# Modulation tiles ahead of a unit's sums, the next weight tile's split behind its second, and RMS statistics that go along with their sums

## Chip, cores and metric

One NeuronCore of a Trainium2 chip runs the whole program. The metric is the device time of one execution in microseconds (us). The kernel before took 2876.29 us, the median of three runs (2874.13 to 2876.8).

## What is computed

Two transformer layers over 512 latent tokens and 256 context tokens of width 1024, then a third layer of another kind (gated linear attention, mLSTM, S5 and a gated feed-forward). Only the first two layers matter here. Everything is float32 at the interface.

```python
for i in range(2):
    mod_lat = silu(c) @ w_ada[i] + b_ada[i]        # 6 x 1024, for x
    mod_ctx = silu(c_ctx) @ w_ada[i] + b_ada[i]    # 6 x 1024, for xc
    h_lat = x * (1 + sc_a) + sh_a;  h_ctx = xc * (1 + csc_a) + csh_a
    # i == 0: q, k, v = split(h @ w_qkv); q, k rms-normed by head, rotated
    # i == 1: cq, ckv, k_pe = split(h @ w_in)
    #         q = rms_norm(cq) @ w_uq;  k, v = rms_norm(ckv) @ w_ukv
    x = layer_norm(alpha * x + g_a * (attention(...) @ w_o))
    x = layer_norm(alpha * x + g_m * (relu(modulated(x) @ w1) ** 2 @ w2))
    # the same two lines for xc where i == 0
```

The third layer's modulation, `silu(c_2) @ ada_w_2`, is computed beside the MLPs of the first two.

## The kernel before

Activations lie with features on the partitions and tokens in the columns, in segments: segment 0 is the 512 latent tokens, segment 1 the 256 context tokens, 2 and 3 are the halves of segment 0. The layer norms go by thirds of 256 tokens, p = 2, 3, 1 in this order.

**Products.** A float32 product is made of three bf16 products (`mm3`, lines 288 to 290): both operands are split into a high and a low bf16 half. Weights come in tiles of 1 MB, [128, 8 x 256]. `load_tiles` (SyncE, line 250) issues their DMAs in the order in which TensorE uses the tiles, into two staging slots of `WS`. `high_halves` (ScalarE, line 274) copies a tile to bf16, `low_halves` (VectorE, line 284) makes the difference, into two pairs of buffers `WB`. A DMA into a slot waits until the tile two places before it has been used up: for a weight tile that is its low half (`dve_done`), for a modulation tile the matmuls on it (`pe_done`).

**Units.** `sums` (line 299) walks through the units of a product. A unit is one weight tile, two blocks of 128 output features; each block has a sum per segment, 8 x 3 matmuls of 512 or 256 columns. With both segments a unit is four sums, with segment 0 alone two. After each sum `then` is called, where other work of TensorE stands.

**Modulation tiles.** `w_ada` is 3 x 8 tiles of 1 MB per layer, [128, 2048], used in float32 straight from the staging slot (`ada_pe`, line 487): four matmuls each. They are laid beside other products by `BESIDE` (line 529): two tiles per unit in the q, k, v product, in `wo0` and in the first MLP's first product `("w1", 0)`, one per unit in `("w1", 1)`. `beside_pe` uses one behind the unit's first sum and one behind its second. When eight tiles are summed, ScalarE copies the rows (`ada_act`, line 496), TensorE transposes them (`ada_turn_pe`, line 502, behind the sum after the last tile) and VectorE adds the bias (line 512).

**Places of the splits.** `next_tiles(tag, i)` names the first weight tile behind unit i. ScalarE and VectorE ask for it before they touch the unit's first sum: in the q, k, v product (`first` in `qkv_act` and `qkv_dve`, ScalarE's square at line 685), and in the MLP (`mlp_act`, relu at 1365 and square at 1367; `mlp_dve`, lines 1377 and 1380). VectorE also computes small tables for the third layer there, one piece behind each sum (`beside(e)` of `mlp_dve`, `tables_dve`). GpSimd fills larger ones from them and stores each with a DMA (`e_scratch`).

**Output products with layer norm.** `wo0`, `w20`, `wo1`, `w21` (attention output and second MLP product of layers 0 and 1) go through `out_sums_pe`, `out_sums_act`, `out_sums_dve`. Their last unit (features 6 and 7) goes by thirds. For each third, `late(p)` and `final(p)` add up mean and mean square in TensorE (lines 1052 to 1064), which need VectorE's `gate(6, p)` and `gate(7, p)` (line 1204). `first_sums_pe` is the first unit of the product that follows; it goes by thirds too, k by k as VectorE delivers the modulated inputs.

**Compressed q, k, v.** `mla_in_pe` makes the sums of cq (three), ckv (four) and k_pe (two). Then it rotates k_pe (`rope_pe`, line 1656) and sums the squares of the seven blocks with a matrix of ones (line 1566). ScalarE turns each of the three sums into a root (lines 1590 and 1592), VectorE scales (line 1611) and splits (line 1615). The next product's first part `qpe` needs the three blocks of cq; ScalarE's `rope_act` (line 1664) starts each of its rotations.

```python
BESIDE = {"qkv": ([("ada0", t) for t in range(8, 16)], 2, 4, "side5"),
          "wo0": ([("ada0", t) for t in range(16, 24)], 2, 4, "side5"),
          ("w1", 0): ([("ada1", t) for t in range(24)] + [("ada2", t) for t in range(8)], 2, 4, "side"),
          ("w1", 1): ([("ada2", t) for t in range(8, 24)], 1, 2, "side")}
```

Of the kernel before, what the change touches and what calls it, by code (L numbers as in the profile page):

```python
# [129 lines left out]
def build(nc, a, out):  # L130
    ctx = ExitStack()
    with ctx:
# [166 lines left out]
        def sums(e, tag, src, units, nks, rhs, segs, then=None, whole=False, ring="dense", first=0):  # L299

            for i, (c0, nc_, ms) in enumerate(units):
# [221 lines left out]
        def first_mods_dve(e):  # L523
# [5 lines left out]
        BESIDE = {"qkv": ([("ada0", t) for t in range(8, 16)], 2, 4, "side5"),  # L529
                  "wo0": ([("ada0", t) for t in range(16, 24)], 2, 4, "side5"),  # L530
                  ("w1", 0): ([("ada1", t) for t in range(24)] + [("ada2", t) for t in range(8)], 2, 4, "side"),
                  ("w1", 1): ([("ada2", t) for t in range(8, 24)], 1, 2, "side")}

        def beside_sum(stage, n):

            if stage not in BESIDE:
                return None, None
            ts, per, sums, _ = BESIDE[stage]
            unit, r = divmod(n, sums)
            name, t = ts[unit * per + per - 1] if unit * per < len(ts) else (None, 0)  # L540
            return ts[unit * per + r] if name and r < per else None, (name, t // 8) if r == per and t % 8 == 7 else None
# [8 lines left out]
        def beside_act(e, stage, n):  # L550
            tile_, _ = beside_sum(stage, n)
            if tile_ and tile_[1] % 8 == 7:
                ada_act(e, tile_[0], tile_[1] // 8)

        def beside_dve(e, stage, n):
            _, whole = beside_sum(stage, n)
            if whole:
                ada_dve(e, *whole)
# [68 lines left out]
        def qkv_pe(e):  # L627
# [13 lines left out]
            def then(e, key, s):  # L641
                u = QU.index((key, s))
                if u > 1:
                    swap(u - 2)
                if u > 0:
                    head(u - 1)
                beside_pe(e, "qkv", u)
# [2443 lines left out]
```

## Time and profile before

| | |
|---|---|
| median of three runs | 2876.29 us |
| profiled execution, its own time | 2874.26 us |
| span of its trace | 2872.5 us |
| mean granted TensorE clock | 0.962 |
| TensorE busy | 2607.8 us, 91% |
| VectorE, ScalarE, GpSimd busy | 50%, 36%, 26% |
| HBM | 92 GB/s over the span |

The profile is one execution. "Busy" for TensorE counts overlapping matmuls once, with modelled ends. The clock is a share of 2.4 GHz. A row of the timeline is "start, duration, engine, line, operation", and in brackets how long the engine had been idle before it and which instruction released it. Such stretches lie, in us of the span: q, k, v product 58 to 232; attention 0 to 449; `wo0` to 533; first MLP's first product to 848 (its first unit is that by thirds), its second to 1118; compressed q, k, v to 1175; attention 1 with its heads to 1436; `wo1`, second MLP to 1827; the third layer to the end.

### The profile page before, as it was taken

The numbers are of one execution on the slowest core, as the hardware profiler recorded it, in microseconds if no ns is written. First come the engines' busy times: TensorE is split into PE (matmuls) and PEld (weight loads), VectorE is DVE, ScalarE is ACT, GpSimd is POOL, SyncE is SP. The second block draws the span as 40 slices with busy tenths as digits, with TensorE's granted clock in tenths as the row PEclk, the third lists the DMA queues.
The fourth block names the chain that finished last, engine by engine and source line by source line (L and its number), as shares of the span: only waits on it lengthen the run. The fifth ranks groups of instructions, "written<-read, shape, count | busy, mean of one in ns | idle before, by whom it ended". The sixth has DMA issues, their size and how long they took to land.

```text
span 2872.5 us, 39059 instructions
## 1 busy us (share of the span) xinstructions
PE 2607.8 (91%) x16373; PEld 1442.9 (50%) x16584; DVE 1445.7 (50%) x2179; ACT 1041.1 (36%) x1713; POOL 743.6 (26%) x985
## 2 busy tenths in 40 slices
PE   4789999889999998889999999887898998899997
PEld 1346665645556576357654445544543333344443
DVE  2336884773342125688664422665765653433322
ACT  2335773333231113567543322322342213422221
POOL 1220000248787722400040000033253543011100
PEclk7899999999999999999999999999989999999998
DMA  6220003345552221210035532221112323233321
GB/s 222 103 88 16 2 2 118 115 160 189 197 176 84 93 75 49 67 59 2 30 118 186 189 109 90 78 96 52 52 52 73 99 70 110 59 103 103 99 96 55
DMA packets 206078, 268.26 MB, mean 93 GB/s; under 512 B 8975, under 2 KB 188558, under 8 KB 196686
## 3 DMA queue, kind: packets, MB, share of 16 engines
q1 hardware_dynamic: 199758, 243.97, 26.5%
q0 software_dynamic: 5280, 18.64, 1.8%
q8 instruction: 130, 2.13, 0.3%
q10 hardware_dynamic: 864, 3.15, 0.3%
q14 instruction: 46, 0.38, 0.0%
HBM read 252.62 MB, written 10.49 MB: 92 GB/s over the span
## 4 chain that ended last, share of the span: by engine, by line
PE 69%; DVE 16%; ACT 5%; issue 3%; POOL 3%; DMA 3%; SPq 0%; POOLq 0%; DVEq 0%; ACTq 0%
PE PS L289 19%; PE PS L288 19%; PE PS L290 19%; DVE WB L284 2%; PE PS L487 2%; PE PS L851 2%; DVE SM L933 2%; DVE AR L939 2%; ACT WB L274 1%; DMA WS<-in_mlp_w 1%; DMA WS<-in_gqa_w_qkv 1%; DVE X L1216 1%; DVE GT L1225 1%; PE PS L632 1%; PE PS L1999 1%
## 5 line engine op out<-in xcount | busy, mean ns | idle before, releaser
L289 PE MATMUL PS<-H,WB 128*128 128x512 bf16 (+1 forms) x1953 | 686.2, 351 | 30.5 <-DVE WB L284 10.5
L288 PE MATMUL PS<-H,WB 128*128 128x512 bf16 (+2 forms) x1907 | 668.2, 350 | 25.5 <-DVE WB L284 13.7
L290 PE MATMUL PS<-H,WB 128*128 128x512 bf16 (+2 forms) x1949 | 683.5, 351 | 1.2
L284 DVE TENSOR_TENSOR WB<-WS,WB 128x2048 bf16<-128x2048 f32 (+3 forms) x165 | 375.5, 2276 | 583.4 <-ACT WB L274 583.3
L274 ACT ACTIVATE WB<-WS 128x2048 bf16<-128x2048 f32 (+3 forms) x165 | 295.5, 1792 | 663.5 <-PE PS L290 424.9
L288 PE MATMUL PS<-AR,WB 128*128 128x512 bf16 (+1 forms) x1279 | 431.6, 337 | 15.8 <-DVE WB L284 7.6
L289 PE MATMUL PS<-AR,WB 128*128 128x512 bf16 (+1 forms) x1280 | 431.7, 337 | 8.1 <-DVE AR L1615 4.8
L290 PE MATMUL PS<-AR,WB 128*128 128x512 bf16 (+1 forms) x1281 | 431.7, 337 | 1.1
L288 PEld LDWEIGHTS PS<-H,WB 128*128 128x128 bf16 x1976 | 194.4, 98 | 298.5 <-issue 65.2
L290 PEld LDWEIGHTS PS<-H,WB 128*128 128x128 bf16 x1976 | 195.2, 99 | 176.4 <-issue 9.2
L289 PEld LDWEIGHTS PS<-H,WB 128*128 128x128 bf16 x1976 | 194.9, 99 | 165.5 <-issue 7.7
L1304 POOL TENSOR_TENSOR X<-X,STAT 128x256 f32<-128x256 f32 x56 | 47.1, 877 | 710.8 <-DVE H L1233 710.8
L288 PEld LDWEIGHTS PS<-AR,WB 128*128 128x128 bf16 x1300 | 127.9, 98 | 135.8 <-issue 13.8
L290 PEld LDWEIGHTS PS<-AR,WB 128*128 128x128 bf16 x1300 | 127.9, 98 | 98.8 <-issue 2.5
L289 PEld LDWEIGHTS PS<-AR,WB 128*128 128x128 bf16 x1300 | 127.9, 98 | 97.3 <-issue 3.3
L939 DVE TENSOR_TENSOR AR<-PS,AR 128x384 bf16<-128x384 f32 x288 | 143.9, 535 | 18.0 <-ACT AR L899 16.8
L933 DVE TENSOR_REDUCE SM<-PS 128x1 f32<-128x768 f32 x160 | 135.5, 848 | 24.4 <-PE PS L290 21.8
L899 ACT ACTIVATE AR<-PS 128x384 bf16<-128x384 f32 x288 | 124.4, 477 | 57.1 <-PE PS L851 55.7
L289 PE MATMUL PS<-AR 128*128 128x64 bf16 (+3 forms) x736 | 142.9, 245 | 2.4 <-ACT STAT L892 0.9
L290 PE MATMUL PS<-AR 128*128 128x64 bf16 (+3 forms) x736 | 142.9, 245 | 0.0
L288 PE MATMUL PS<-AR 128*128 128x64 bf16 (+3 forms) x705 | 131.7, 240 | 4.8 <-ACT AR L892 2.1
L1204 DVE SCALAR_TENSOR_TENSOR X<-PS,MOD,X 128x256 f32<-128x256 f32 (+1 forms) x56 | 33.5, 597 | 189.9 <-PE PS L290 189.9
(399 smaller groups left out, 3781.3 us busy)
## 6 DMA issues: line engine op xcount, KB each, us to landing
WS<-in_mlp_w SPq DMA_DIRECT2D x64, 1024.0 KB, 5.6
WS<-in_w_ada SPq DMA_DIRECT2D x48, 1024.0 KB, 5.0
WS<-in_w_in SPq DMA_DIRECT2D x26, 1024.0 KB, 5.1
WS<-in_ada_w SPq DMA_DIRECT2D x24, 1024.0 KB, 4.9
WS<-in_ffn_w_in SPq DMA_DIRECT2D x44, 512.0 KB, 4.8
e_scratch<-EB POOLq DMA_DIRECT2D x16, 512.0 KB, 3.7
EB<-e_scratch POOLq DMA_DIRECT2D x16, 512.0 KB, 3.6
WS<-in_ffn_w_out SPq DMA_DIRECT2D x8, 1024.0 KB, 5.4
```

Of the source, the lines that this page charges most:

```text
L274: e.activation(halves_of(i)[0], staged(i), COPY).then_inc(ac.sem, ac.mark(("hi", i)))
L284: e.tensor_tensor(lo, staged(i), hi, SUB).then_inc(dv.sem, dv.mark(("lo", i)))
L288: e.matmul(out_, l[0], r[0], start=start, stop=False)
L289: e.matmul(out_, l[0], r[1], start=False, stop=False)
L290: return e.matmul(out_, l[1], r[0], start=False, stop=stop)
L487: m = e.matmul(ps(bank_of[name, "sums", g], 512, slice(32 * j, 32 * j + 32)), SIL[:, pair, k, :], v[:, 0, j * 512:(j + 1) * 512], start=k ...
L851: m = e.transpose(at(("T", t, u, i), 128, (k - a_) * 128), Q.p(u)[:, k * 128:(k + 1) * 128], ident)
L899: e.activation(Q.pt(u, i)[0], Q.turned_at(u, i), COPY).then_inc(ac.sem, ac.mark(("high", t, u, i)))
L933: e.tensor_reduce(Q.largest(u), Q.scores_at(u), AX.X, MAX, negate=True).then_inc(dv.sem, dv.mark(("max", t, u)))
L939: e.tensor_tensor(lo, Q.turned_at(u, i), hi, SUB).then_inc(dv.sem, dv.mark(("low", t, u), ("free", ("T", t, u, i))))
L1204: e.scalar_tensor_tensor(out=seg(X, f, s), in0=ps(bank_of[tag, f, s], SEG[s][1]), scalar=MOD[:, i, (3 * j + 2) * 8 + f, SEG_OF[s]:SEG_OF[s ...
L1304: e.tensor_tensor(seg(X, f, p), seg(X, f, p), factor_at(p), MUL).then_inc(po.sem, po.mark(("over", tag, f, p), ("factor read", tag)))
```

## The change

Six edits:

1. In `sums`, both modulation tiles of a unit are taken and used ahead of its first sum; the transposes of a finished set stand behind the first sum of the same unit. The order of the tiles in the staging slots stays as it was.
2. ScalarE and VectorE split the next weight tile behind the unit's second sum (its first, where a unit has two).
3. In the last unit of `w20`, `wo1` and `w21`, the next tile's split stands ahead of `gate(7)` and of ScalarE's `part_sums`.
4. `late(1)` and `final(1)` of the last third leave `out_sums_pe`; `first_sums_pe` of the next product runs them (`rest`) behind the fourth k of its first third.
5. `gate(6)` of the next third stands behind three of eight `less_mean`, `gate(7)` two features sooner.
6. The seven sums of squares go between the sums of ckv and k_pe; the root of cq, its scaling and its split come behind the fourth block, those of ckv behind the rotation's start.

```diff
@@ sums
                     w, hi, lo = tile(e, (tag, i, c), src[k0 * 128:(k0 + nk) * 128, c0:c0 + nc_], nk, nc_, whole)
+                    if beside and c == 0:
+                        beside_pe(e, beside, i)
@@ BESIDE, helpers
-        def beside_pe(e, stage, n):
-            tile_, whole = beside_sum(stage, n)
-            if tile_:
-                ada_pe(e, *tile_, BESIDE[stage][3])
-            if whole:
-                ada_turn_pe(e, *whole, BESIDE[stage][3])
+        def beside_pe(e, stage, unit):
+            for tile_ in beside_tiles(stage, unit):
+                ada_pe(e, *tile_, BESIDE[stage][2])
+
+        def beside_turn_pe(e, stage, unit):
+            for whole in whole_set(stage, unit):
+                ada_turn_pe(e, *whole, BESIDE[stage][2])
@@ qkv_act, first (qkv_dve likewise)
-                high_halves(e, next_tiles("qkv", key // 2))
+                if u % 4 == 0:
+                    beside_act(e, "qkv", u // 4)
                 pe.wait_ge(e, ("qkv", key, s))
...
                 e.activation(sq, ps(bank_of["qkv", key, s], n), SQUARE).then_inc(ac.sem, ac.mark(("sq", u)))
-                beside_act(e, "qkv", u)
+                if u % 4 == 1:
+                    high_halves(e, next_tiles("qkv", key // 2))
@@ out_sums_pe
-                        if key == 7:
+                        if key == 7 and p != 1:
                             late(p)
                             final(p)
                 k0 += nk
+            def rest(e):
+                if ns > 1:
+                    late(1)
+                    final(1)
+            return rest
@@ first_sums_pe
+                    if p == 2 and k == 3:
+                        rest(e)
@@ out_sums_act
-                high_halves(e, next_tiles(tag, i, last))
-                beside_act(e, tag, n)
+                high_halves(e, through(tag, i, last))
...
+                if n % (2 * len(segs)) == len(segs) - 1:
+                    high_halves(e, next_tiles(tag, i, last))
             high_halves(e, through(tag, 3, last))
+            beside_act(e, tag, 3)
             square(6, P[0])
+            if tag != "wo0":
+                high_halves(e, next_tiles(tag, 3, last))
             part_sums(0)
             square(7, P[0])
@@ out_sums_dve
             gate(6, P[0])
-            gate(7, P[0])
+            beside_dve(e, tag, 3)
             if tag != "wo0":
                 low_halves(e, next_tiles(tag, 3, last))
+            gate(7, P[0])
...
                 for f in range(8):
                     less_mean(f, p)
-                if after:
-                    gate(6, after)
+                    if f == 2 and after:
+                        gate(6, after)
...
-                    if f == 2 and after:
+                    if f == 0 and after:
                         gate(7, after)
@@ mlp_act (mlp_dve likewise)
-                high_halves(e, next_tiles(("w1", i), t))
+                if n % (2 * len(segs)) == 0:
+                    beside_act(e, ("w1", i), t)
...
-                beside_act(e, ("w1", i), n)
+                if n % (2 * len(segs)) == len(segs) - 1:
+                    high_halves(e, next_tiles(("w1", i), t))
@@ mla_in_pe
+            first_sums_pe(e, "cq", WI, CQ[0], (0,), "w20", rest, lambda: None)
             linear(e, "cq", WI, CQ, [8], h_of("w20"), (0,), first=1)
-            linear(e, "ckv", WI, CKV, [8], h_of("w20"), (0, 1))
-            linear(e, "kpe", WI, KPE, [8], h_of("w20"), (0, 1))
+            square(0)
+            square(1)
+            behind = iter(range(2, 6))
+            linear(e, "ckv", WI, CKV, [8], h_of("w20"), (0, 1), lambda e, m, s: square(next(behind)))
+            linear(e, "kpe", WI, KPE, [8], h_of("w20"), (0, 1), lambda e, m, s: square(6) if s == 0 else None)
```

**TensorE, one unit of the first MLP's first product.** L288 to L290 are the sums (512 columns, then 256), L487 before and L489 after the change are the matmuls on modulation tiles. Before:

```order
L290 MATMUL PS<-H,WB 128x512
L487 MATMUL PS<-WS,SIL 32x512 [waits weights1_landed]
L487 MATMUL PS<-WS,SIL 32x512 x3
L288 MATMUL PS<-H,WB 128x256
...
L290 MATMUL PS<-H,WB 128x256
L487 MATMUL PS<-WS,SIL 32x512 [waits weights0_landed]
L487 MATMUL PS<-WS,SIL 32x512 x3
L288 MATMUL PS<-H,WB 128x512 [waits act_done]
```

After:

```order
L290 MATMUL PS<-H,WB 128x256
L489 MATMUL PS<-WS,SIL 32x512 [waits weights0_landed]
L489 MATMUL PS<-WS,SIL 32x512 x3
L489 MATMUL PS<-WS,SIL 32x512 [waits weights1_landed]
L489 MATMUL PS<-WS,SIL 32x512 x3
L288 MATMUL PS<-H,WB 128x512
```

The second modulation tile's wait for its landing moved from behind two sums to ahead of both.

**SyncE, the same stage.** One unit's three loads; these rows read the same before and after.

```order
L263 DMA WS<-in_mlp_w 128x8x256 [waits pe_done]
L263 DMA WS<-in_w_ada 128x2048 [waits pe_done]
L263 DMA WS<-in_w_ada 128x2048 [waits dve_done]
```

The second modulation tile's load waits for VectorE (`dve_done`), whose place in its own program moved.

**ScalarE, the same stage.** L274 is the split, L1365 and L1367 are relu and square before, L1391 and L1393 after. Before:

```order
L274 ACTIVATE WB<-WS 128x2048 [waits weights1_landed]
L1365 ACTIVATE GT<-PS 128x512 [waits pe_done,dve_done]
L1367 ACTIVATE AR<-GT 128x512 [waits act_done]
L1365 ACTIVATE GT<-PS 128x256 [waits pe_done,dve_done]
L1367 ACTIVATE AR<-GT 128x256 [waits act_done]
```

After:

```order
L1391 ACTIVATE GT<-PS 128x512 [waits pe_done,dve_done]
L1393 ACTIVATE AR<-GT 128x512 [waits act_done]
L1391 ACTIVATE GT<-PS 128x256 [waits pe_done,dve_done]
L1393 ACTIVATE AR<-GT 128x256 [waits act_done]
L274 ACTIVATE WB<-WS 128x2048 [waits weights1_landed]
```

The split went from ahead of the unit's first relu to behind its second square.

## Rows read from the trace of the kernel before

**Rows 1.** Busy time by stretch: start:end, us, each engine busy (instructions), clock, DMA share, GB/s

```profile
94.50:186.00 91.50, 72.66 (x370) 36.03 (x376) 29.80 (x40) 29.33 (x52) 22.45 (x19) 0.91 0.31 104
627.00:848.00 221.00, 213.41 (x1333) 115.44 (x1356) 87.12 (x121) 69.83 (x112) 170.35 (x323) 1.00 0.58 190
```

**Rows 2.** Timeline, one unit of q, k, v: SyncE, ScalarE, TensorE

```profile
101.93 0.38 SPq L263 DMA_DIRECT2D WS<-in_gqa_w_qkv  x1
...
106.98 1.91 ACT L274 ACTIVATE WB<-WS 128x2048 bf16<-128x2048 f32 x1 [2.97 <-DMA WS<-in_gqa_w_qkv]
...
109.52 1.72 PE L632 MATMUL PS<-AR,KM 128*128 128x512 f32 x2 [4.92 <-ACT AR L685]
111.17 1.93 PE L487 MATMUL PS<-WS,SIL 128*32 128x512 f32 x8
...
123.53 0.67 PE L632 MATMUL PS<-AR,KM 128*128 128x512 f32 x1 [1.13 <-ACT AR L685]
```

**Rows 3.** Waits of TensorE over the span: who <- whom, us in total, times, longest

```profile
PE PS L632 <- ACT AR L685: 22.9, 9, 5.0
...
PE PS L502 <- ACT STAT L496: 5.8, 5, 1.9
```

**Rows 4.** Busy time by stretch, behind a long and a short wait; the clock is third from last

```profile
109.50:113.30 3.80, 3.58 (x10) 0.62 (x12) 3.02 (x4) 1.77 (x4) 1.99 (x1) 0.55 0.00 0
123.50:128.00 4.50, 4.42 (x18) 2.04 (x20) 1.85 (x4) 2.01 (x4) 0.67 (x1) 1.00 0.00 0
```

**Rows 5.** Timeline, the join of wo0 and the first MLP

```profile
537.89 1.22 PE L1054 MATMUL PS<-X,KM 128*128 128x256 f32 x2 [5.00 <-DVE X L1204]
...
534.45 0.33 SPq L263 DMA_DIRECT2D WS<-in_w_ada  x1
```

**Rows 6.** Busy time by stretch: one unit of the first MLP's first product

```profile
644.50:662.30 17.80, 17.59 (x112) 9.54 (x112) 6.63 (x9) 4.90 (x8) 13.46 (x29) 1.00 0.58 200
```

**Rows 7.** Timeline of ScalarE: relu and square of 256 columns, then the next relu

```profile
562.47 0.38 ACT L1365 ACTIVATE GT<-PS 128x256 f32<-128x256 f32 x1 [1.91 <-PE PS L290]
562.88 0.42 ACT L1367 ACTIVATE AR<-GT 128x256 bf16<-128x256 f32 x1
563.20 0.58 ACT L1365 ACTIVATE GT<-PS 128x512 f32<-128x512 f32 x1
```

**Rows 8.** Timeline of VectorE and SyncE; two loads of modulation tiles, us to landing last

```profile
659.68 2.29 DVE L284 TENSOR_TENSOR WB<-WS,WB 128x2048 bf16<-128x2048 f32 x1 [10.86 <-ACT WB L274]
...
662.00 0.33 SPq L263 DMA_DIRECT2D WS<-in_w_ada  x1
...
WS<-in_w_ada SPq DMA_DIRECT2D x1, 1024.0 KB, 4.9
...
WS<-in_w_ada SPq DMA_DIRECT2D x1, 1024.0 KB, 5.5
```

**Rows 9.** Timeline of TensorE and VectorE where VectorE computes tables

```profile
587.42 0.61 PE L288 MATMUL PS<-H,WB 128*128 128x512 bf16 x1 [5.60 <-DVE WB L284]
...
587.29 0.68 DVE L1377 TENSOR_TENSOR GT<-GT 128x512 f32<-128x512 f32 x1
...
591.79 0.59 DVE L1380 TENSOR_TENSOR AR<-GT,AR 128x256 bf16<-128x256 f32 x1
```

**Rows 10.** Timeline of TensorE behind the sums of compressed q, k, v

```profile
1162.79 4.82 PE L1566 MATMUL PS<-GT,KM 128*128 128x512 f32 x10
...
1175.10 0.63 PE L289 MATMUL PS<-AR,WB 128*128 128x512 bf16 x1 [4.76 <-DVE AR L1615]
```

**Rows 11.** Timeline of VectorE and TensorE at wo1's layer norm

```profile
1448.35 2.29 DVE L284 TENSOR_TENSOR WB<-WS,WB 128x2048 bf16<-128x2048 f32 x1 [2.28 <-ACT WB L274]
...
1474.09 0.28 PE L288 MATMUL PS<-H,WB 128*128 128x256 bf16 x1 [2.17 <-DVE H L1233]
```

**Rows 12.** A load on the chain (start, us); issues of the page: KB, median us to landing

```profile
724.56 7.73 DMA WS<-in_mlp_w
...
WS<-in_mlp_w SPq DMA_DIRECT2D x64, 1024.0 KB, 5.6
...
e_scratch<-EB POOLq DMA_DIRECT2D x16, 512.0 KB, 3.7
```

More of the change, by code:

```diff
@@ L297, in groups, with sums @@
             return [(i, key, s) for i, (_, _, ms) in enumerate(units) for key, _, _ in ms for s in segs]
-        def sums(e, tag, src, units, nks, rhs, segs, then=None, whole=False, ring="dense", first=0):
+        def sums(e, tag, src, units, nks, rhs, segs, then=None, whole=False, ring="dense", first=0, beside=None):
             for i, (c0, nc_, ms) in enumerate(units):
@@ L525, in first_mods_dve @@
             low_halves(e, 1 + next((i for i, t in enumerate(tiles) if not t[3]), 0))
[L529 to L541, printed above, removed]
@@ new lines, in beside_tiles, with whole_set @@
+        def beside_tiles(stage, unit):
+            ts, per, _ = BESIDE.get(stage, ((), 0, None))
+            return ts[unit * per:unit * per + per]
+        def whole_set(stage, unit):
+            return [(name, t // 8) for name, t in beside_tiles(stage, unit) if t % 8 == 7]
+        def beside_pe(e, stage, unit):
[4 more added lines that the diff above has]
+                ada_turn_pe(e, *whole, BESIDE[stage][2])
@@ L558, in beside_dve, with beside_act @@
+        def beside_act(e, stage, unit):
+            for whole in whole_set(stage, unit):
+                ada_act(e, *whole)
+        def beside_dve(e, stage, unit):
+            for whole in whole_set(stage, unit):
                 ada_dve(e, *whole)
@@ L1027, in out_sums_pe @@
             P, ns = PARTS[segs], len(segs)
[L1028 removed]
+            n_ = iter(range(6 * ns))
             def shift(s):
@@ L1158, in out_sums_act @@
                 part_sums(1)
-            for n in range(6 * len(segs), 6 * len(segs) + 2 * len(P)):
-                beside_act(e, tag, n)
-            if tag != "wo0":
-                high_halves(e, next_tiles(tag, 3, last))
             for i, p in enumerate(P):
@@ L1337, in hid_at, with mlp_pe, then @@
             return hid[:, 0, m, o0:o0 + n], hid[:, 1, m, o0:o0 + n]
-        def mlp_pe(e, i, segs, tag):
+        def mlp_pe(e, i, segs, tag, rest):
             per = 2 * len(segs)
-            def beside():
-                for n in range(per):
-                    beside_pe(e, ("w1", i), n)
             n = iter(range(per, len(W1) * per))
-            first_sums_pe(e, ("w1", i), a["mlp_w1"][i], W1[0], segs, tag, beside, "dense" if i else "five")
-            linear(e, ("w1", i), a["mlp_w1"][i], W1, [8], h_of(tag), segs, lambda e, m, s: beside_pe(e, ("w1", i), next(n)), first=1)
+            def then(e, m, s):
+                unit, r = divmod(next(n), per)
+                if r == 0:
+                    beside_turn_pe(e, ("w1", i), unit)
+            first_sums_pe(e, ("w1", i), a["mlp_w1"][i], W1[0], segs, tag, rest, lambda: beside_pe(e, ("w1", i), 0), "dense" if i else "five")
+            linear(e, ("w1", i), a["mlp_w1"][i], W1, [8], h_of(tag), segs, then, first=1, beside=("w1", i))
             def rhs(e, k, s):
@@ L1558, in mla_in_pe, with root_act @@
             pe.at["h read: mla"] = pe.n
             rope_pe(e, "kpe", 0)
[L1560 to L1566 removed]
+        def root_act(e, name):
+            _, parts, count, _, o = next(r for r in RMS if r[0] == name)
+            w = SEG[parts[0][1]][1]
+            pe.wait_ge(e, ("rms", max(n for n, p in enumerate(RMS_PARTS) if p[0] == name)))
+            e.activation(STAT[o][:, 0:w], ps(bank_of["rms", name], w), LN, bias=epsc, scale=1.0 / count).then_inc(ac.sem, ac.mark(("free", ("rms", name))))
+            ac.wait_ge(e)
+            e.activation(STAT[o][:, 0:w], STAT[o][:, 0:w], EXP, scale=-0.5).then_inc(ac.sem, ac.mark(("rstd", name)))
```

144 lines of the change are left out of this document (76 added, 68 removed).

## The prediction

> **What bounds the kernel now.** I read the page first (TensorE is busy for 91% of the span), then the table by stage, the waits of TensorE, and the timelines of the three stages that the change touches. In the q, k, v stage TensorE works 72.7 of 91.5 us; in the first MLP's first product it works 213 of 221 us, at full clock [rows 1]. So there is much to win in the first place and little in the second, where the question is what a new wait would cost.
>
> In the q, k, v stage one of the waits returns in every unit of four sums. ScalarE's program has the split of the next weight tile ahead of the first sum's square. That tile's DMA is issued at 101.93, when TensorE has used the modulation tile that stands behind the unit's first sum; it lands 5 us later, ScalarE splits it for 1.91 us from 106.98, and only then squares the sum. TensorE, which wants that square for the head matmul, has been idle for 4.92 us [rows 2]. All waits of that kind sum to 22.9 us in nine pieces [rows 3]: five of 1.0 to 5.04 us at the head of a unit, and four of 0.7 to 1.2 us in a unit's second half. Behind the long one the granted clock is 0.55 for 3.8 us, behind the 1.13 us one it stays at 1.00 [rows 4]. The Trainium skill, "TensorE: Matmul & The Clock Gate", section "HAM oscillation", says that waits for a DMA between short pieces of matmul work make the engine fall to its low clock again each time; the trace agrees for the 5 us waits (1.2 GHz behind them), not for the 1 us ones.
>
> **The change, part by part.** *q, k, v.* Both modulation tiles are used ahead of the unit's first sum, so the DMA of the next weight tile starts a sum earlier, and its split stands behind the second square, where ScalarE has time until the third sum ends. The half unit without a split shows what is left: from 113.1 to 124.6 it takes 11.45 us, with its own wait of 1.13 us [rows 2]. That wait will stand in both halves (no modulation tile covers it any more). A unit is then 2 x 11.45 and 2 tiles of 0.95 us, 24.9 us with an issue gap, against 91.5/3 = 30.5 [rows 1]: 5.6 x 3 = 16.8 us less. The first unit waits for its modulated inputs anyway and gives about 1.8; the last loses most of one such wait, 2.4. Together **-21 us**. The new load behind the split lands in time here: head matmul at 10.3, its two activations, square and split to 15.0, DVE to 17.3, landing to 22.5, while TensorE wants it 23.9 us after the unit's sums began.
>
> *Output product of attention 0.* Same two edits. A unit lasts about 17.9 us up to its second modulation tile; that tile's load waits for VectorE's half of the split, which ends 14.0 us in (sum ends 8.7, gate, square, split, DVE), and lands at 19.2. Two of the three changes of unit meet this: **+2.5 us**.
>
> *The join to the first MLP.* The last third's statistics (its mean and mean square) move from behind its sums into the next product, behind four of eight rows of the first part. The wait of 5.00 us [rows 5] goes. But both modulation tiles stood ahead of that product already, and the second is issued at 534.45 [rows 5], behind VectorE's split. It lands at 539.6, later than TensorE now gets there (532), so the engine idles seven microseconds instead of five, and its statistics come behind 2.7 us of sums. I get VectorE's start on the MLP 2.3 us later.
>
> *The first MLP's first product, where the new wait is.* Tiles lie in two staging slots, in the order weight, modulation, modulation, weight. So the second modulation tile of a unit takes the slot of that unit's weight tile, and its DMA waits until that weight tile is split. Before, it was wanted behind the unit's second sum; now it is wanted ahead of the first. And the split, which stood before the first relu of the unit ahead, now stands behind the second. That makes a loop through five engines. From the start of a unit's sums: two sums, (17.8 - 2.0)/2 = 7.9 us by the unit of 17.8 us [rows 6]; relu and square of 256 columns 0.8 [rows 7]; ScalarE's split 1.9 [rows 2]; VectorE's 2.3, from 659.68 until the issue at 662.00; landing 4.9 to 5.5, I take 5.2 [rows 8]; the tile itself 1.0. Sum 19.1 us, against 17.8 for the work alone: 1.3 us of wait per unit.
>
> The first units are worse, because VectorE also computes the tables for the last layer there, a piece of them behind each sum. TensorE waited 5.60 us at 587.42 for the split of unit 2's weight tile. Now VectorE first does two more sums and the table pieces between, 587.29 to 592.38, which is 5.1 us [rows 9]. Then comes a DMA of 5.1 and a modulation tile at the low clock, 1.9. With the 2.3 from the join, unit 2's sums start at 587.3 + 5.1 + 2.3 + 5.1 + 1.9 = 601.7, against 587.4 + 1.9 = 589.3 with its tiles counted: 12.4 us late. Unit 3 adds 1.0, eleven more units 11 x 1.3 = 14.3. The last unit has none behind it (-1.3), three waits of 1.9 us and less for the transposes of the modulations go [rows 3] (-4.0), and some loads will land later than 5.2 (+0.6). **+23 us**, in a stage that had hardly any idle time.
>
> *Second MLP.* One modulation tile per unit; the slot order differs (weights in one slot, modulations in the other) and I find 0.5 us of slack. Nothing, bounds 0 and +4 (0.3 us in half of the units).
>
> *Statistics of compressed q, k, v.* Seven squares were summed by TensorE behind all sums: 12.3 us from 1162.79 to the next product at 1175.10, the last 4.76 of them a wait for VectorE [rows 10]. Now they stand between the sums. Five of them, three of 1.0 us at 512 columns (the x10 of the row is five matmuls, each listed twice) and two of half that at 256, add 4.2 us; two fill a wait for a weight tile. From the end of the sums to the q product's rotated part, the chain on ScalarE and VectorE is about 6.5 us shorter by its instructions, but the next product's rotation, not its first matmul, ends that chain, so no more than that comes back. With 1.5 us for VectorE's split in front of a gate in the product before, less 0.8 for ScalarE's squares ahead of a split: **-3 us** (bounds +3 and -8).
>
> *Product of attention 1.* The same split in front of the gate: at 1448.35 it stood ahead of the variance, having waited 2.28 us for ScalarE's half, and TensorE still waits 2.17 us for VectorE 25 us later [rows 11]. **-1.5 us**.
>
> Sum: -21 + 2.5 + 23 - 3 - 1.5 = 0. The profiled execution took 2874.3 us, 2.0 under the median of the runs. So I forecast **2876.5 us**: a gain in one stage and a loss in another that cancel. [...]
>
> **The rivals.** *Faster: the second modulation tile is not late.* If the loop closes within 17.8 us in the first MLP (a landing of 4 us or less, or an earlier split), the 11 x 1.3 us go: 2876.5 - 14 = 2862. If the lateness of unit 2 isn't there either, 2850. For it: VectorE is busy only 87 of 221 us in the stage [rows 1]. Against it: no landing of a modulation tile that I read there is under 4.9 us [rows 8], and the order rows show the wait. *Slower: landings count now, and GpSimd's transfers lengthen them.* GpSimd stores 16 tables of 512 KB from this stage on, eight of them by my count between units 4 and 15, and one load of a weight tile took 7.73 us until ScalarE could use it, where 5.6 is the median [rows 12]. Hidden before, such 2.1 us would come on top of the loop: 8 x 2.1 = 17, so 2893.5. It decides if more than one load in three meets a store. The Trainium skill, "DMA: Bandwidth & Descriptors", section "Issuing engines are not separate DMA queues", says that transfers of all issuers run on the same 16 engines and interleave, which speaks for it; by it each meeting lengthens a load. *The first gain is smaller:* the change doesn't do what it says in the q, k, v stage, because the wait moves from a unit's head to its second half, as the 1.13 us ones [rows 2] became part of each half. If 3 us per unit stay, 2888.
>
> **How the numbers follow.** A difference under 0.2% (5.8 us) can't be told from none here. The forecast has 0.60, with its own range 2866 to 2887 (the bounds of its small terms); 0.36 of it lies within 0.2%, 0.11 faster, 0.13 slower. The late tile that isn't late has 0.19, all faster. The lengthened landings have 0.14 and the smaller gain 0.07, all slower. That gives faster 0.30, same 0.36, slower 0.34. The range reaches into both neighbours: 2853 to 2896.
>
> **What would show it.** In the changed profile: units of some 25 us in q, k, v, with waits of 1.1 us before the head matmuls and the clock near 1.00; units of 19 us in the first MLP, with TensorE waiting 1 to 1.5 us for a DMA of in_w_ada ahead of each; one idle stretch of some 18 us there at the second unit's end; no wait of 4.76 us before the compressed q product, but one before its first rotation. I am wrong if the MLP's units stay at 17.8 us (then the time is near 2850), or if the q, k, v units stay above 27 us.

## The result and the profile after

The changed kernel took 2889.08 us (median of five runs, 2885.87 to 2894.38), the kernel before 2876.42 us (five runs, 2874.13 to 2880.12). The ratio is 1.0045 with a 95% interval of 1.003 to 1.006: slower by 12.7 us. I had forecast 2876.5 within 2853 to 2896, so the time lies in the range, but on the side to which I gave 0.34, and 2 us outside the 2866 to 2887 that the forecast itself had.

| | after |
|---|---|
| profiled execution, its own time | 2894.38 us |
| span of its trace | 2892.6 us |
| mean granted TensorE clock | 0.960 |
| TensorE busy | 2605.9 us, 90% |
| VectorE, ScalarE, GpSimd busy | 50%, 36%, 25% |

The profiled execution is the longest of the five, 5.3 us above their median. What follows in its trace adds up to the span's difference (20.1 us), not to the median's. The runs below, each with a trace of its own, say what of it is typical.

**The q, k, v stage.** The busy table of one unit (start:end, us, each engine busy, clock, DMA share, GB/s):

```profile
117.33:141.92 24.59, 22.12 (x123) 11.85 (x124) 9.90 (x14) 9.59 (x17) 6.18 (x6) 1.00 0.37 129
```

A unit's sums start 24.6 us behind those of the unit ahead, against 30.5 before [rows 1], at full clock. TensorE's timeline, the waits of one unit, and one wait in the stage's fourth unit that I had not foreseen:

```profile
102.91 1.10 PE L634 MATMUL PS<-AR,KM 128*128 128x512 f32 x2 [1.13 <-ACT AR L689]
...
114.22 1.10 PE L634 MATMUL PS<-AR,KM 128*128 128x512 f32 x2 [1.13 <-ACT AR L689]
...
151.99 1.11 PE L504 MATMUL PS<-KM,STAT 128*128 128x128 f32 x4 [3.65 <-ACT STAT L498]
```

The 1.13 us wait stands in both halves, as forecast; the 4.92 us one [rows 2] is gone. L504 are the transposes of the finished modulation rows. They stand behind the unit's first sum, and ScalarE copies those rows only behind two steps of its own: one waits, by way of VectorE and GpSimd, for TensorE's `swap`, the other for its `head`, and TensorE runs both after that same sum. TensorE's first attention matmul starts 19.5 us sooner than before (213.19 against 232.65).

**The join to the first MLP.** TensorE's timeline, then VectorE's:

```profile
520.29 1.93 PE L489 MATMUL PS<-WS,SIL 128*32 128x512 f32 x8 [3.61 <-DVE WB L284]
...
527.00 1.94 PE L489 MATMUL PS<-WS,SIL 128*32 128x512 f32 x8 [4.78 <-DMA WS<-in_w_ada]
528.87 0.40 PE L288 MATMUL PS<-H,WB 128*128 128x256 bf16 x1
...
533.37 0.60 PE L1059 MATMUL PS<-EB,KM 128*128 128x256 f32 x2
```

```profile
536.50 0.42 DVE L1297 TENSOR_TENSOR STAT<-PS,STAT 128x256 f32<-128x256 f32 x1 [5.02 <-ACT STAT L1189]
```

The same two places before (TensorE's first sum, VectorE's variance of the last third), and the second modulation tile's load on the chain that ended last after the change:

```profile
546.86 0.28 PE L288 MATMUL PS<-H,WB 128*128 128x256 bf16 x1
```

```profile
545.80 0.42 DVE L1272 TENSOR_TENSOR STAT<-PS,STAT 128x256 f32<-128x256 f32 x1
```

```profile
520.26 6.69 DMA WS<-in_w_ada
```

The 5.00 us wait [rows 5] became two, 8.4 us in all. The MLP's first sums start at 528.87, 18.0 us sooner than before (546.86). But the last third's variance (L1297) comes 7.6 us behind that start, where before (545.80) it came 1.1 us ahead of it. So VectorE has this third 8.7 us later against the sums than before. Counted from the last sum ahead of the join (its last matmul starts at 532.18 before, 516.41 after), the sums start 2.2 us sooner and VectorE has the third 6.5 us later.

**The first MLP's first product.** TensorE at its second unit's end:

```profile
583.20 1.94 PE L489 MATMUL PS<-WS,SIL 128*32 128x512 f32 x8 [13.79 <-DVE WB L284]
...
588.05 1.94 PE L489 MATMUL PS<-WS,SIL 128*32 128x512 f32 x8 [2.92 <-DMA WS<-in_w_ada]
```

This is the idle stretch of some 18 us that I had named (16.7, and both tiles at the low clock). From there on the chain of waits reads like the loop of the prediction. Its pieces over one unit (start, us, what), with TensorE's sums left out:

```profile
648.63 1.07 PE PS L489 x8
...
657.70 0.39 ACT GT L1391
658.12 0.42 ACT AR L1393
658.53 1.81 ACT WB L274
660.36 2.30 DVE WB L284
662.68 4.97 DMA WS<-in_w_ada
667.70 1.07 PE PS L489 x8
```

Second tile and two sums 9.07, relu and square 0.83, ScalarE's split 1.83, VectorE's 2.32, landing 5.02: 19.07 us from one second modulation tile to the next. Over twelve units, busy table:

```profile
607.71:842.81 235.10, 214.93 (x1334) 117.36 (x1357) 91.56 (x146) 72.05 (x111) 162.06 (x328) 0.99 0.53 180
```

That is 19.6 us per unit, against 221.02 / 12 = 18.4 over the same twelve before (transposes included). Of the clock, three windows behind waits of 1.66, 2.11 and 2.54 us for a DMA:

```profile
610.44:614.40 3.96, 3.80 (x21) 1.54 (x23) 2.67 (x13) 0.60 (x1) 0.00 (x0) 1.00 0.99 338
...
805.57:809.50 3.93, 3.60 (x13) 0.99 (x15) 0.00 (x0) 0.00 (x0) 1.12 (x7) 0.57 0.91 272
...
764.66:768.60 3.94, 3.60 (x13) 0.99 (x15) 0.00 (x0) 0.60 (x1) 3.39 (x13) 0.57 0.90 260
```

The granted clock stays at 1.00 (2.4 GHz) behind the first and falls toward 1.2 GHz behind the other two. The Trainium skill, "TensorE: Matmul & The Clock Gate", section "HAM oscillation", has an example in which waits for a DMA of about 3 to 5 us bring the low clock back each time. In this stage 2.11 and 2.54 us were enough for that, and the waits of 1.05 to 1.66 us left the clock alone.

**Second MLP.** TensorE and VectorE, two units of two sums each:

```profile
1516.44 1.07 PE L489 MATMUL PS<-WS,SIL 128*32 128x512 f32 x8 [0.37 <-DVE WB L284]
...
1528.33 1.07 PE L489 MATMUL PS<-WS,SIL 128*32 128x512 f32 x8 [0.35 <-DVE WB L284]
```

```profile
1525.99 2.29 DVE L284 TENSOR_TENSOR WB<-WS,WB 128x2048 bf16<-128x2048 f32 x1 [0.97 <-ACT WB L274]
```

A unit takes 11.89 us, with a wait of 0.35 us in each of them for VectorE's split, which ends at 1528.28.

**Compressed q, k, v.** TensorE at the join ahead of it and at the rotation:

```profile
1145.27 0.63 PE L289 MATMUL PS<-H,WB 128*128 128x512 bf16 x1 [6.80 <-DVE GT L1248]
...
1193.49 1.19 PE L1703 MATMUL PS<-GT,KM 128*128 128x512 f32 x1 [5.46 <-ACT GT L1711]
```

The wait of 4.76 us [rows 10] is gone and one of 5.46 stands before the first rotation, as forecast. From the MLP's end to here the stage takes as long as before, within 0.1 us.

### The profile page after: what moved, and what is told of

The parts are those of the page before. It is cut to its first block, busy times and chain, and to the rows that moved or that the text cites. A ratio compares the mean times of both kernels' runs of the same rounds, so it can differ in the third digit from the quotient of the medians.

```text
span 2892.6 us, 39059 instructions
## 1 busy us (share of the span) xinstructions
PE 2605.9 (90%) x16373; PEld 1447.1 (50%) x16584; DVE 1449.1 (50%) x2179; ACT 1045.3 (36%) x1713; POOL 733.2 (25%) x985
## 4 chain that ended last, share of the span: by engine, by line
PE 65%; DVE 17%; ACT 7%; DMA 4%; POOL 3%; issue 3%; SPq 0%; POOLq 0%; DVEq 0%; ACTq 0%
PE PS L289 18%; PE PS L288 18%; PE PS L290 17%; DVE WB L284 4%; DMA WS<-in_w_ada 3%; ACT WB L274 3%; PE PS L858 2%; DVE SM L940 2%; PE PS L489 2%; DVE AR L946 2%; DMA WS<-in_ada_w 1%; DVE GT L1248 1%; DVE X L1239 1%; PE PS L2046 1%; PE PS L876 1%
## 5 line engine op out<-in xcount | busy, mean ns | idle before, releaser
L290 PE MATMUL PS<-H,WB 128*128 128x512 bf16 (+2 forms) x1949 | 686.3, 352 | 1.3
L288 PE MATMUL PS<-H,WB 128*128 128x512 bf16 (+2 forms) x1908 | 671.6, 352 | 17.3 <-DVE H L1256 5.6
L288 PE MATMUL PS<-AR,WB 128*128 128x512 bf16 (+1 forms) x1281 | 432.4, 338 | 16.1 <-DVE WB L284 7.6
L274 ACT ACTIVATE WB<-WS 128x2048 bf16<-128x2048 f32 (+3 forms) x165 | 294.9, 1788 | 392.1 <-PE PS L290 378.5
L290 PE MATMUL PS<-AR,WB 128*128 128x512 bf16 (+1 forms) x1279 | 430.9, 337 | 1.0
L288 PEld LDWEIGHTS PS<-H,WB 128*128 128x128 bf16 x1976 | 195.7, 99 | 271.8 <-issue 51.1
L290 PEld LDWEIGHTS PS<-H,WB 128*128 128x128 bf16 x1976 | 196.2, 99 | 177.6 <-issue 9.6
L288 PEld LDWEIGHTS PS<-AR,WB 128*128 128x128 bf16 x1300 | 127.7, 98 | 132.5 <-issue 14.9
L290 PEld LDWEIGHTS PS<-AR,WB 128*128 128x128 bf16 x1300 | 127.8, 98 | 98.7 <-issue 2.8
L1403 DVE TENSOR_TENSOR GT<-GT 128x512 f32<-128x512 f32 x96 | 62.4, 650 | 223.1 <-ACT GT L1391 223.1
L1391 ACT ACTIVATE GT<-PS 128x512 f32<-128x512 f32 x96 | 50.4, 525 | 318.6 <-PE PS L290 289.8
L489 PE MATMUL PS<-WS,SIL 128*32 128x512 f32 x576 | 87.3, 688 | 73.9 <-DMA WS<-in_w_ada 37.8
L946 DVE TENSOR_TENSOR AR<-PS,AR 128x384 bf16<-128x384 f32 x288 | 143.8, 535 | 18.4 <-ACT AR L906 17.0
L289 PE MATMUL PS<-AR 128*128 128x64 bf16 (+3 forms) x736 | 143.6, 245 | 2.4 <-ACT STAT L899 0.9
```

Source lines behind the costliest of these rows:

```text
L274: e.activation(halves_of(i)[0], staged(i), COPY).then_inc(ac.sem, ac.mark(("hi", i)))
L288: e.matmul(out_, l[0], r[0], start=start, stop=False)
L289: e.matmul(out_, l[0], r[1], start=False, stop=False)
L290: return e.matmul(out_, l[1], r[0], start=False, stop=stop)
L489: m = e.matmul(ps(bank_of[name, "sums", g], 512, slice(32 * j, 32 * j + 32)), SIL[:, pair, k, :], v[:, 0, j * 512:(j + 1) * 512], start=k ...
L946: e.tensor_tensor(lo, Q.turned_at(u, i), hi, SUB).then_inc(dv.sem, dv.mark(("low", t, u), ("free", ("T", t, u, i))))
```

## The experiments

Each ratio is to runs of the kernel before that were taken beside it (their medians: 2874.8 us for e1 to e4, 2874.1 for e5 to e8, 2875.4 for e9 to e12), with its 95% interval.

**e1, the q, k, v edits alone, on the kernel before.**

```diff
@@ sums
+                    if beside:
+                        for r in range(2):
+                            beside_pe(e, beside, 4 * i + r)
@@ qkv_act, first (qkv_dve likewise)
-                high_halves(e, next_tiles("qkv", key // 2))
...
+                if u % 4 == 1:
+                    high_halves(e, next_tiles("qkv", key // 2))
```

> The kernel before with the edits of the q, k, v stage alone (both modulation tiles ahead of a unit's sums, the split behind the second square). By the two traces this stage gave 19.5 us at attention's first matmul and the attention gave 1.3 of it back, so I expect 2857 to 2858 us against 2876.4, ratio 0.9935. Rival: the gain only moves waits on, into the output product or the join to the MLP (where an engine other than TensorE is late), then 2865 to 2876.

Measured: 2855.80 us, 0.9934 [0.9921, 0.9947], 19.0 us faster than before. The stage's gain reaches the end whole; it does not turn into waits further on. So what the changed kernel lost elsewhere is some 32 us.

**e2 to e4: the two edits of the first MLP's first product, taken apart.** The loop needs both: tiles wanted ahead of the sums, and a split behind the second. e2 takes both back, e3 only the split, e4 only the tiles.

```diff
@@ e3: mlp_act (mlp_dve likewise); e2 has this too
             for n, (t, m, s) in enumerate(groups(W1, segs)):
+                if i == 0:
+                    high_halves(e, next_tiles(("w1", i), t))
...
-                if n % (2 * len(segs)) == len(segs) - 1:
+                if i != 0 and n % (2 * len(segs)) == len(segs) - 1:
                     high_halves(e, next_tiles(("w1", i), t))
@@ e4: mlp_pe; e2 has this too
+                if i == 0:
+                    behind_pe(e, ("w1", i), m_, 4, 2)
```

(`behind_pe` uses one tile behind the first sum, one behind the second, and the transposes behind the third; ScalarE's copy of the rows and VectorE's bias move with them. e2 has all of this too.)

> The changed kernel with tiles and split of the first MLP's first product back in their old places; the join in front of it keeps its edit. Loop theory: the 1.7 us of wait per unit and the exposed landings go, but VectorE still starts on the MLP 8.7 us later than its sums would allow, because the last third's statistics stand behind the late modulation tile, and unit 2 waits for that. The stage cost 32.5 us, so 24 come back: 2865 us. Rival one, the join costs nothing: all 32.5 come back, 2857. Rival two, GpSimd's stores or the DMA queues make the stage longer whatever the places are: 2880 or more.

> The changed kernel with only the split of the first MLP's first product back ahead of the unit's first relu; the tiles stay in front. Loop theory: the split now ends some 10.7 us into the unit, the second modulation tile lands at 15.9 and is wanted at 16.8, so the loop is open and units take 17.8 us again without a wait; at unit 2 the late VectorE (8.7) and one exposed landing (5) stay: 2870 us. Rival: tiles in front cost by themselves (each waits for a landing or brings the low clock), then units stay at 19 us or more and the time near 2887.

> The changed kernel with only the tiles of the first MLP's first product back behind the first and second sum; the split stays behind the second square. Loop theory: the second tile is wanted 9 us later than in the changed kernel and lands in time, the split ends at 16.2 of 17.8 us, so units take 17.8 us; at unit 2 VectorE's tables stand ahead of the split (5.1) and it starts late (8.7): 2870 us. Rival: the late split alone is the cost, because ScalarE and VectorE then end behind TensorE: units of 19 us or more, 2885 or more.

Measured: e2 2867.89 us, 0.9977 [0.9967, 0.9986]; e3 2872.16 us, 0.9997 [0.9987, 1.0006]; e4 2866.11 us, 0.9968 [0.9956, 0.9980]. Against 1.0045 for the change, each edit taken back alone brings most of what both bring (e3 0.48%, e4 0.77%, e2 0.68%). In none of the three does TensorE wait as long as 0.8 us for a modulation tile from unit 3 on. The rival of tiles that cost by themselves falls with e3, that of a split that is simply too late with e4. TensorE's waits at unit 2, of e2, e3 and e4 in this order:

```profile
575.18 0.61 PE L288 MATMUL PS<-H,WB 128*128 128x512 bf16 x1 [9.47 <-DVE WB L284]
```

```profile
573.55 1.94 PE L489 MATMUL PS<-WS,SIL 128*32 128x512 f32 x8 [8.76 <-DVE WB L284]
...
578.44 1.94 PE L489 MATMUL PS<-WS,SIL 128*32 128x512 f32 x8 [2.95 <-DMA WS<-in_w_ada]
```

```profile
581.53 0.61 PE L288 MATMUL PS<-H,WB 128*128 128x512 bf16 x1 [14.56 <-DVE WB L284]
```

From 9.47 to 14.56 is the 5.1 us of two sums with their table pieces on VectorE [rows 9]; e3 shows the exposed landing apart from it. With e4 the waits for the transposes of the modulation rows stay away, as in the changed kernel. They are there in e2 (0.75 to 2.48 us) and in e3 (2.04, 2.23, 2.16 and 1.58 us), because ScalarE's early split stands in front of the copy of the rows:

```profile
678.91 0.66 PE L504 MATMUL PS<-KM,STAT 128*128 128x128 f32 x4 [2.23 <-ACT STAT L498]
```

**e5, the statistics of the last third back ahead of the tiles.**

```diff
@@ out_sums_pe
-                        if key == 7 and p != 1:
+                        if key == 7 and (p != 1 or tag == "wo0"):
                             late(p)
                             final(p)
@@ rest
-                if ns > 1:
+                if ns > 1 and tag != "wo0":
```

> The changed kernel with the last third's mean and mean square of the first output product taken back from the middle of the MLP's first sums to their old place, ahead of the modulation tiles. Theory: VectorE gets the variance some 8 us earlier, TensorE starts its sums 1 to 2 us later at most, since the late modulation tile ends the wait either way; unit 2 of the MLP then waits 8 us less for VectorE. 2889 - 8 + 1.5 = 2882.5 us. Rival: the 5 us wait that the change removed comes back in full in front of the tiles and nothing is won, 2889 or more.

Measured: 2884.11 us, 1.0035 [1.0024, 1.0046]. By the medians 5 us less than the change; the ratios are 0.1% (2.9 us) apart and their intervals overlap, so the total time alone does not show a gain. The traces are clearer. TensorE, then VectorE:

```profile
519.32 1.22 PE L1061 MATMUL PS<-X,KM 128*128 128x256 f32 x2 [4.90 <-DVE X L1227]
...
575.61 1.94 PE L489 MATMUL PS<-WS,SIL 128*32 128x512 f32 x8 [13.87 <-DVE WB L284]
```

```profile
528.90 0.42 DVE L1297 TENSOR_TENSOR STAT<-PS,STAT 128x256 f32<-128x256 f32 x1
```

This run was 2.7 us ahead of the changed kernel's already before the join (VectorE's split there starts at 515.25 and 517.95). The variance comes 7.6 us sooner, 4.9 with that taken off, and unit 2's tile too (583.20 to 575.61). The 5 us wait is back, but the modulation tile lands while it and the statistics last, so nothing is lost by it: the sums start at 525.78, 0.4 us sooner than in the changed kernel. That leaves 4.9 us as the price of the moved statistics at unit 2, by one trace of each kernel, against the 6.5 I expected.

**e6, the transposes of the q, k, v stage behind the second sum.**

```diff
@@ qkv_pe, then (beside_dve in qkv_dve likewise)
-                if u % 4 == 0:
+                if u % 4 == 1:
                     beside_turn_pe(e, "qkv", u // 4)
```

> The changed kernel with the transposes of the modulation rows of the q, k, v stage behind the second sum of their unit instead of the first. Theory: ScalarE copies the rows only behind a step that waits for TensorE's own swap matmul, so the transposes behind the first sum wait 3.65 us; behind the second sum that wait is gone: 2885.5 us, no wait over 1.5 us at the transposes. Rival: the wait moves to the head matmul next to it, 2889.

Measured: 2883.80 us, 1.0027 [1.0019, 1.0036]. The 3.65 us wait is gone; the longest in its place is a head matmul's:

```profile
152.23 1.10 PE L634 MATMUL PS<-AR,KM 128*128 128x512 f32 x2 [1.61 <-ACT AR L689]
```

From the same head matmul (89.64 in the changed kernel, 89.29 here) to the same attention matmul (216.48, 211.55) it is 4.6 us less than in the changed kernel.

**e7, the split of the second MLP early again, the tile still in front.** The edit is that of e3 with `i == 1`.

> The changed kernel with only the second MLP's split back ahead of a unit's first relu (two sums a unit, the modulation tile stays in front). Theory: there the chain first sum, relu, square, split on ScalarE, split on VectorE ends 0.35 us behind TensorE in each unit, units take 11.9 us instead of 11.5; with the split early they take 11.5 again: 15 x 0.43 = 6.4 us less, 2882.5 us. Rival: the modulation tile in front is what costs, units stay at 11.9 us and the time at 2889.

Measured: 2880.57 us, 1.0025 [1.0016, 1.0034]. TensorE's timeline has the tiles 11.46 us apart, with no wait:

```profile
1504.14 1.07 PE L489 MATMUL PS<-WS,SIL 128*32 128x512 f32 x8
...
1515.60 1.06 PE L489 MATMUL PS<-WS,SIL 128*32 128x512 f32 x8
```

So 0.43 us per unit came from the late split alone. By the ratios this is 5.8 us.

**e8, GpSimd's stores cut to a sixteenth.** It leaves the last layer's tables incomplete.

```diff
@@ tables_pool (the load in the last layer likewise)
-                e.dma_start(EDR[r], E_.rearrange("p a n -> p (a n)"))...
+                e.dma_start(EDR[r, :, 0:64], E_.rearrange("p a n -> p (a n)")[:, 0:64])...
```

> The changed kernel, but GpSimd stores and later loads only 64 of each table's 1024 columns, so each store moves 32 KB instead of 512 KB (the tables of the last layer are then incomplete). Loop theory: most units lose their 1.2 us to the length of the loop itself; only the two or three units in which a store meets the late modulation tile (20.3 to 21.0 us instead of 19.1) get shorter, 3 to 5 us less in the MLP, 2885. Rival, the stores are the main cost: every unit returns to about 17.8 us and 17 us or more go, 2872 or less. The last layer may gain a little by its shorter loads in both cases.

Measured: 2890.46 us, 1.0053 [1.0040, 1.0066]: not faster, not even by the 3 to 5 us that I expected. Twelve units, of e8 and of e5, which has the full stores:

```profile
605.07:835.54 230.47, 211.98 (x1333) 116.88 (x1356) 91.75 (x146) 72.06 (x111) 170.73 (x332) 1.00 0.49 166
```

```profile
598.83:831.21 232.38, 213.45 (x1334) 117.11 (x1357) 91.48 (x146) 72.03 (x111) 158.46 (x317) 0.99 0.54 182
```

19.2 against 19.4 us per unit. The same twelve take 230.76 us in e6 and 230.57 in e7, which have the full stores too. So the stores were worth 0.1 to 2 us against these three traces. The change's own 235.10 has two long waits at the low clock (2.54 and 2.11 us); e5 has one of 1.95, e8 none over 1.73. That a store lengthened the load behind such a wait is possible, not shown.

**e9, a combination.** The edits of e5, e6 and e7, the tiles of e4, and in the first MLP's first product the split early for units 0 and 1, late from then on:

```diff
@@ mlp_act (mlp_dve likewise)
+            early = (lambda t: t < 2) if i == 0 else (lambda t: True)
             for n, (t, m, s) in enumerate(groups(W1, segs)):
+                if early(t):
+                    high_halves(e, next_tiles(("w1", i), t))
...
-                if n % (2 * len(segs)) == len(segs) - 1:
+                if not early(t) and n % (2 * len(segs)) == len(segs) - 1:
                     high_halves(e, next_tiles(("w1", i), t))
```

> The changed kernel with five repairs at once: the q, k, v turn behind the second sum; the statistics of the first output product's last third back ahead of the tiles; in the first MLP's first product the tiles behind the first and second sum, with the split early for units 0 and 1 and late from then on; in the second MLP the split early. Against before: -19.0 in q, k, v, -3.6 the turn, +1 in the output product, -5 for the modulation turns that no longer wait, -1.5 at the second output product, nothing else: 2874 - 28 = 2846 us, and no wait over 1 us in the MLP's units from 3 on. Rival: units of the MLP wait again because split and landing now meet in another place, or the gains overlap, 2855 or more.

Measured: 2847.03 us, 0.9901 [0.9888, 0.9914], 28 us faster than before and faster than both kernels. TensorE at unit 2, and the busy table of the units behind it:

```profile
566.56 0.61 PE L288 MATMUL PS<-H,WB 128*128 128x512 bf16 x1 [7.63 <-DVE WB L284]
```

```profile
596.00:812.00 216.00, 216.00 (x1369) 116.73 (x1371) 89.50 (x129) 73.38 (x111) 163.16 (x311) 1.00 0.59 194
```

TensorE is busy for all of 216 us.

**e10, e11: two edits of the change taken out of the combination.** e10 has the second output product's statistics (`w20`) in their old place too (`if key == 7:` in the line of e5), e11 the old functions `mla_in_pe`, `mla_in_act` and `mla_in_dve` of the kernel before.

> The combination, with the last third's statistics of the second output product (the MLP's) in their old place too. Theory: behind this join VectorE has no tables to compute, so it isn't late in what follows, and the wait of 6.8 us there is the sum of the smaller ones before (7.9): no difference, within 1.5 us of the combination. Rival: as at the first join the late variance costs 5 us, then 5 less.

> The combination, with the compressed q, k, v stage as it was before the change (all seven sums of squares behind the sums). My prediction gave the new order 3 us; the two traces show 0 over the stage with its join. Theory: 0 to 1 us slower than the combination. Rival, the gain is there but hidden by the join's longer wait in the same stretch: 3 us or more slower.

Measured: e10 2847.97 us, 0.9910 [0.9897, 0.9923]; e11 2852.40 us, 0.9919 [0.9906, 0.9931]. e10 is level with the combination, so at that join the moved statistics cost nothing. That this is because VectorE has no tables behind it is argued, not shown. e11 is 5 us slower by the medians, with intervals that overlap; in the traces, against a common point ahead of the stage, it is 1.9 us late in the products of the heads and 0.6 us late at the first attention matmul. How much of the new order's gain there is, between 0.6 and 5 us, stays open.

**e12, the smallest repair: the split behind the first square, the tiles in front.**

```diff
@@ mlp_act (mlp_dve likewise)
-                if n % (2 * len(segs)) == len(segs) - 1:
+                if n % (2 * len(segs)) == 0:
                     high_halves(e, next_tiles(("w1", i), t))
```

> The changed kernel with one edit: in the first MLP's first product the split stands behind the unit's first square instead of its second, the tiles stay in front. Loop arithmetic: the weight tile lands 6 to 6.6 us into the unit, ScalarE 1.9, VectorE 2.3, landing 5.2: 16.0 us, under the 16.8 at which TensorE wants the tile. So units of 17.8 us without a wait, and VectorE's piece before unit 2's split is one sum shorter: 2889 - 11 x 1.7 - 4 = 2866 us. Rival: the waits shrink only by the 2.1 us of the second sum less what the DMA takes with both tiles on the way, so half of the units still wait, 2878.

Measured: 2861.77 us, 0.9956 [0.9944, 0.9967], some 25 us less than the change by the ratios, for one condition. TensorE at unit 2, and twelve units behind it:

```profile
578.07 1.94 PE L489 MATMUL PS<-WS,SIL 128*32 128x512 f32 x8 [10.36 <-DVE WB L284]
```

```profile
602.67:814.70 212.03, 212.03 (x1358) 118.16 (x1357) 92.08 (x150) 71.05 (x111) 145.66 (x289) 1.00 0.57 196
```

Units take 17.7 us without a wait. The loop is 16 us long by my sum, and TensorE's own work is longer, so the loop no longer counts.

## Why the prediction was right, and where it was wrong

- **q, k, v, -21.** Measured -19.0 (e1), -19.5 by the traces. Units and waits were as forecast. What I missed is the wait of 3.65 us at the transposes: I followed where the split goes on ScalarE, but not what ScalarE's copy of the rows stands behind once the transposes come a sum earlier. Without it (e6, 4.6 us by the traces) the gain would have been 24.
- **Output product of attention 0, +2.5.** Two waits of 0.47 and 0.46 us for the second modulation tile, +0.9. Right place, the size too large.
- **The join, VectorE 2.3 us late.** This is one of the two steps that failed, in its size. My 2.3 us count from the place where TensorE gets to the join; counted so it was 6.5 us. I had the right order of things, but put the landing of the second modulation tile at 539.6, 7.4 us behind the last sum, and 2.7 us for the sums ahead of the statistics. The tile landed 10.5 us behind that sum: its load was issued 1.6 us later than I had it and took 6.69 us instead of about 5, beside the next weight tile's. And behind that wait the sums ran at the low clock (0.50) and took 4.5 us (528.87 to 533.37). These two are 4.9 us, a little more than the 4.2 that were missing. e5 gives the price of the moved statistics by themselves, 4.9 us, all at unit 2.
- **First MLP's first product, +23.** The mechanism is shown: the loop needs both edits (e2 to e4), closes again when it is made shorter than a unit (e12), and has the length I summed, 19.1 us (19.07 in the chain). Unit 2's sums start at 590.32. TensorE gets to the join 15.8 us sooner than before, so before's place, my 589.3, is 573.5 there: they are 16.8 us late, not 12.4, and nearly all of the difference is the join's. In the traces the stage with its join cost 30.3 us (the next product's first statistics start at 916.68 against 902.19, 14.5 later, where 15.8 had been gained), 32.5 counted from its first sums; but the profiled execution is 5.3 us above the median. By the ratios of e2 the two edits cost 19.6 us, with the 4.9 of the join 24.5.
- **Second MLP, 0 (bounds 0 and +4).** The other step that failed. I found 0.5 us of slack where 0.35 us were missing: first sum, relu, square, both halves of the split take longer than the two sums. 15 units by 0.43 us are 6.4 us, outside my bounds (e7: 5.8).
- **Compressed q, k, v, -3.** The waits moved as I said, but by the traces nothing came back; by e11 somewhere between 0.6 and 5 us did. Not settled. (The five squares that I put at 4.2 us make 4.0 by their own lengths.)
- **wo1, -1.5.** From attention 1 to the third layer the trace lost 4.7 us; less the 6.4 of the second MLP that is -1.7, as forecast.
- **The rivals.** The tile was late, so the first fell. Stores that lengthen landings fell as a main cost with e8. The smaller first gain was true in kind (a wait came in), at 3.65 us in all and not 3 per unit. That its 2888 is the number nearest to the measured time is a coincidence.

From medians and ratios: -19.0 (e1), +19.6 (e2), +4.9 (e5's trace), +5.8 (e7) and +0.9 make 12.2 us, against 12.7 measured. That is closer than the parts are known: `wo1` (-1.7) and compressed q, k, v (0 to -5) are not in it. My sum was 0. Against the measured parts it lacks 5.8 us at the second MLP, 2.0 in q, k, v and 1.5 in the first MLP with its join (24.5 against 23, where a join that was mis-sized by 4.2 is partly made up by the rest), and it has 1.6 too much at the output product; the other 4.5 are the -3 and -1.5, of which at least the -1.5 was real. So the sign was lost at the second MLP first of all, and not on the loop. "Slower" should have had more than 0.34: each place at which I took a small slack or lateness (join, second MLP) had its open end on the slow side.

## What to carry to other kernels

When loads of two kinds share staging slots, write down for each load whose slot it takes and what frees that slot, and walk the loop from the wanted tile back to itself: if its length is over the work of one round, the excess is paid in every round, and one step moved by one sum can be worth 25 us (e12). Moving a step earlier in one engine's program also moves everything that now stands behind its wait: ask for the statistics, the copy, the transposes behind it, and follow them to the engine with no slack. Here that was VectorE with its tables, and a delay of 4.9 us at a join was still whole at unit 2, some 50 us later.

## What the runs showed of the hardware

In the first MLP the granted clock stayed at 1.00 behind waits for a modulation tile of up to 1.73 us (e8, at 684.66 us). It fell behind one of 1.95 us (e5, at 774.79 us: 0.56 in the mean of the next 3.9 us, so mostly 1.2 GHz), and that makes such a wait cost twice: the tile behind it took 1.90 us instead of 1.07. But no one length divides the two. Behind a wait of 2.25 us (e7, at 795.99 us) the tile took 1.06 us, at a clock of 1.00. Behind the same wait of 3.6 us at the join it took 1.06 or 1.07 us in five traces (e2, e4, e6, e8, e12) and 1.93 or 1.94 us in three (the change, e3, e7). And behind the same wait of 4.90 us there (`gate`, ahead of the statistics), the two modulation tiles that follow the statistics took 1.92 us together in e9 and 3.64 us in e10.

The same 1 MB load, of the join's second modulation tile, took 4.9 us to land where no other ran beside it (before, issued at 534.45 us) and 6.69 us where the next weight tile's was issued 2.0 us behind it (the change, from 520.26 us). Sixteen times smaller stores by GpSimd beside loads of 1 MB changed a unit by 0 to 0.2 us (e8 against e7, e6 and e5).

VectorE's operations on 16 columns (the tables) took 0.58 or 0.65 us each while GpSimd worked through its `TENSOR_TENSOR` instructions (550.03 to 567.74 in the change, 559.34 to 577.06 before), and 0.20 to 0.42 us, most of them 0.20 or 0.27, while it worked through the `TENSOR_SCALAR` instructions behind them. So VectorE's work ahead of unit 2's tile is longer than its instruction count says. What of unit 2's wait this makes, no run here tells.

The same code ahead of the join varied by 2 to 3 us from run to run (e9 to e11 pass the same matmul at 515.35, 517.57 and 516.61, e5 was 2.7 us ahead of the changed kernel), so differences of that size between single traces had to be taken from a common point.
